# A decoder trunk's state-space scan: real sums on GpSimd, imaginary sums and scans on VectorE

## The chip, the cores and the metric

The kernel runs on one core of a Trainium2 chip. The metric is the device time of one execution in microseconds (us), lower is better; the number given for a kernel is the median of its runs. One execution was also taken by the hardware profiler, and all rows below come from that one.

## What is computed

The reference is a decoder trunk of two layers on 512 tokens of width 1024. Each layer projects its input for three token mixers that stand side by side (windowed attention, a gated delta rule, and a diagonal state space called S5), sums what they give, and then runs an expert network and a gated embedding. The edit is inside S5. There the projected input `u` drives 16 groups of 64 complex states, each with a complex decay:

```python
bu_r = jnp.einsum('blgp,gnp->blgn', uf, bb_r)
bu_i = jnp.einsum('blgp,gnp->blgn', uf, bb_i)
xr, xi = jax.vmap(scan_one)(bu_r, bu_i)      # x[t] = a * x[t-1] + bu[t], complex, along the tokens
y = (jnp.einsum('blgn,gpn->blgp', xr, c_re) - jnp.einsum('blgn,gpn->blgp', xi, c_im) + d_skip * uf)
```

## The kernel before

The states stand on partitions, 128 at a time, which makes 8 blocks a layer (`S5_BLOCKS`); the 512 tokens stand along the free dimension. The hardware's scan is real, and the decay is complex. So the kernel turns the inputs of every token by the angle that the decay has gathered up to it (a table `m.rot`, cosine and sine, made on GpSimd in the phase before), scans the real and the imaginary half separately with the decay's magnitude `m.mag`, and turns the result back.

All of this is in `phase_attend`, together with the windowed attention, with which it shares the engines. The attention has 16 iterations (`N`); its VectorE part is `soft` (L767 to L781): three operations that read scores from PSUM banks (L772, L775, L777) and a maximum (L781). VectorE's order is written out by hand (L822 to L833): `soft(it)`, in some iterations a normalisation, a copy or a skip (L819), and at every odd iteration from 3 to 17 one recurrence, `recur(b)`, for the blocks 0 to 7. The last two recurrences have no `soft` between them. TensorE's order is written out likewise (L700 to L712): the scores one iteration ahead, transposed probabilities, the inputs of a block (`s5_input`, L676), the attention's values, and the outputs of a block (`s5_output`, L683, matmul L688) at the iteration after its recurrence on VectorE. After block 3 and after block 7, VectorE adds the skip term to the finished outputs (L819). ScalarE copies a block's inputs from PSUM to `bu` (L745, L747). GpSimd sets a tile of zeros to zero (L727) and has nothing else in this phase. An all-engine barrier (`clear`) ends the phase.

`recur(b)` has two halves of the same build. In the first, `turn` makes four products of 128x512 in two instructions (L795) into the tile `turned`; L803 adds the real half and L804 subtracts the imaginary half into `ur`; a signal (L805) frees `bu` for ScalarE; then both halves are scanned, the real one first (L807). In the second, `turn` runs on the scanned `z` into the same tile `turned`, L813 and L814 make the two halves of `xs`, and a signal (L815, semaphore `x_ready`) frees TensorE's outputs. `recur(b)` waits for that signal of block b - 1 before it overwrites `turned`.

`step.mark` lets an instruction count up a semaphore when it is done, `step.step` does so and waits for the count, and `sem_inc` is an instruction of its own in the engine's queue that counts up a semaphore for another engine. All tiles are float32 with 128 partitions. The sums and products of a recurrence read two tensors from SBUF each; L772 reads a table of distances from SBUF and the scores from PSUM.

Of the kernel before, what the change touches and what calls it, by code (L numbers as in the profile page):

```python
# [20 lines left out]
ALU = mybir.AluOpType  # L21
# [18 lines left out]
S5_BLOCKS = 8  # L40
# [92 lines left out]
def over(ap, shape):  # L133

    return ap.to_broadcast(list(shape))


def semaphores(m, names):

    names = names.split()  # L140
    while len(m.sems) < len(names):
        m.sems.append(m.ctx.enter_context(m.nc.semaphore(f"phase{len(m.sems)}")))
    return namedtuple("Semaphores", names)(*m.sems[:len(names)])
# [9 lines left out]
COMMON = "landed0 landed1 landed2 params_in act_filled act_read vec_filled vec_read act_step vec_step pool_step"  # L153
# [435 lines left out]
def phase_attend(m, layer):  # L589
# [3 lines left out]

    nc, io = m.nc, m.io
    with ExitStack() as ctx:
        s = semaphores(m, COMMON + " soft_ready exp_done o_filled o_ready ur_ready scanned x_ready y_done y_read gelu_done zeros_set cells_cleared")
        sb = lambda n, shape, dt=F32: ctx.enter_context(nc.sbuf_tensor(f"{n}_{layer}", shape, dt))
        small = sb("small2", [P, 64])
        zeros = sb("zeros", [P, ZEROS])
# [1 line left out]
        ur = sb("s5_ur", [P, 2, T])  # L601
        z = sb("s5_z", [P, 2, T])
        turned = sb("s5_turned", [P, 2, 2, T])
        xs = sb("s5_x", [P, 2, 2, T])
# [24 lines left out]
        def _(pe):  # L629
# [51 lines left out]
                bu_count[b] = to_act.n  # L681

            def s5_output(b):  # L683
                pe.wait_ge(s.x_ready, b + 1)
                if b == 4:
                    pe.wait_ge(s.y_read, 1)
                for part in range(2):
                    ins = nc.tensor.matmul(ybank[:, :], m.s5_out[:, part, b * P:(b + 1) * P], xs[:, b % 2, part, :],  # L688
                                           start=(b % 4 == 0 and part == 0), stop=(b % 4 == 3 and part == 1))
                ins.then_inc(s.y_done, 1)  # L690
# [34 lines left out]
        @block.gpsimd  # L725
        def _(pool):
            nc.gpsimd.memset(zeros[:, :], 0.0).then_inc(s.zeros_set, 1)  # L727

        @block.scalar
        def _(act):  # L730
# [30 lines left out]
        @block.vector  # L761
        def _(v):
            step = Link(v, s.vec_step)
            banks = Reader(v, m.banks[3:6], s.vec_filled, s.vec_read)
            tt, stt = nc.vector.tensor_tensor, nc.vector.scalar_tensor_tensor

            def soft(it):  # L767
                r, sl = it // 4, it % 4
                if it >= 3:
                    v.wait_ge(s.act_filled, pt_count[it - 3])  # L770
                bank = banks.take()
                stt(out=e[it % 3][:, 0:512], in0=m.c("dist_g0")[:, (3 - r) * P:(7 - r) * P], scalar=-float(SLOPES[sl]),  # L772
                    in1=bank[:, :], op0=ALU.mult, op1=ALU.add).then_inc(s.vec_read, 1)
                bank = banks.take()
                step.mark(stt(out=e[it % 3][:, 512:640], in0=m.c("dist_g1"), scalar=-float(SLOPES[SLOTS + sl]),  # L775
                              in1=bank[:, 0:P], op0=ALU.mult, op1=ALU.add))
                stt(out=e[it % 3][:, 640:768], in0=m.c("dist_g2"), scalar=-float(SLOPES[2 * SLOTS + sl]),  # L777
                    in1=bank[:, P:2 * P], op0=ALU.mult, op1=ALU.add).then_inc(s.vec_read, 1)
                banks.settle()
                step.settle()  # L780
                nc.vector.tensor_reduce(nmax[:, it:it + 1], e[it % 3], AX_X, ALU.max, negate=True).then_inc(s.soft_ready, 1)  # L781

            def normalise(r):
                v.wait_ge(s.o_filled, 4 * r + 4)
                if r >= 2:
                    v.wait_ge(s.act_filled, at_count[r - 2])
                step.step(nc.vector.reciprocal(rden[:, 4 * r:4 * r + 4], den[:, 4 * r:4 * r + 4]))
                tt(osb[r % 2].rearrange("p (s c) -> p s c", s=4),
                   obanks[r % 2][:, 0:256].rearrange("p (s c) -> p s c", s=4),
                   over(rden[:, 4 * r:4 * r + 4].unsqueeze(2), (P, 4, HEAD)), ALU.mult).then_inc(s.o_ready, 1)  # L790

            def turn(b, src):

                for n in range(2):
                    step.mark(tt(turned[:, n], src, over(m.rot[:, n, b, :].unsqueeze(1), (P, 2, T)), ALU.mult))  # L795
                step.settle()

            def recur(b):
                v.wait_ge(s.act_read, bu_count[b])
                if b >= 1:  # L800
                    v.wait_ge(s.x_ready, b)
                turn(b, bu[:, b % 2])
                step.mark(tt(ur[:, 0], turned[:, 0, 0], turned[:, 1, 1], ALU.add))  # L803
                step.step(tt(ur[:, 1], turned[:, 0, 1], turned[:, 1, 0], ALU.subtract))  # L804
                v.sem_inc(s.ur_ready, 1)  # L805
                for part in range(2):
                    nc.vector.tensor_tensor_scan(z[:, part, :], over(m.mag[:, b:b + 1], (P, T)), ur[:, part, :],  # L807
                                                 0.0, ALU.mult, ALU.add).then_inc(s.scanned, 1)
                v.wait_ge(s.scanned, 2 * b + 2)
                if b >= 2:  # L810
                    v.wait_ge(s.y_done, b - 1)
                turn(b, z[:, :, :])
                step.mark(tt(xs[:, b % 2, 0], turned[:, 0, 0], turned[:, 1, 1], ALU.subtract))  # L813
                step.step(tt(xs[:, b % 2, 1], turned[:, 0, 1], turned[:, 1, 0], ALU.add))  # L814
                v.sem_inc(s.x_ready, 1)  # L815

            def skip(yt):
                v.wait_ge(s.y_done, 4 * yt + 4)
                stt(out=m.sT[:, yt, :], in0=m.uT[:, yt, :], scalar=m.s5_d[:, yt:yt + 1], in1=ybank[:, :],  # L819
                    op0=ALU.mult, op1=ALU.add).then_inc(s.y_read, 1)  # L820

            for it in range(N + 4):  # L822
                if it < N:
                    soft(it)
                if it >= 3 and (it - 3) % 4 == 3 and (it - 3) // 4 < 4:
                    normalise((it - 3) // 4)
                if it in (11, 19):
                    skip((it - 11) // 8)
                if it - 1 in GATES_AT:
                    bank = banks.take()  # L830
                    nc.vector.tensor_copy(m.ba[:, GATES_AT.index(it - 1), :], bank[:, 0:2 * DN]).then_inc(s.vec_read, 1)
                if it % 2 == 1 and 0 <= (it - 3) // 2 < S5_BLOCKS:
                    recur((it - 3) // 2)  # L833
# [1301 lines left out]
def decoder_trunk(nc, io):  # L2135
    with ExitStack() as ctx:
# [24 lines left out]
        for layer in range(DEPTH):  # L2161
            with ExitStack() as mix:
# [6 lines left out]
                with ExitStack() as own:  # L2169
                    so = lambda n, shape, dt=F32: own.enter_context(nc.sbuf_tensor(f"{n}_{layer}", shape, dt))  # L2170
                    m.mixer_consts = so("mixer_consts", [P, ALWAYS])
                    m.ba = so("ba", [P, NT, 2 * DN])
                    m.w_ba = so("w_ba", [P, KD, 2 * DN])
                    m.conv_w = so("conv_w", [P, 3 * DN, 4])
                    m.a_log = so("a_log", [P, DN])
                    m.dt_bias = so("dt_bias", [P, DN])
                    m.out_gain = so("out_gain", [P, 1])
                    with ExitStack() as front:
                        sf = lambda n, shape, dt=F32: front.enter_context(nc.sbuf_tensor(f"{n}_{layer}", shape, dt))
                        m.work_a = sf("work_a", [P, NT * D])  # L2180
                        m.qkT = m.work_a[:, :].rearrange("p (b n) -> p b n", b=8)
                        m.att_qk = sf("att_qk", [P, 4, QK_HEADS * HEAD])
                        m.att_v = sf("att_v", [P, 4, SLOTS * HEAD])
                        m.uT = sf("uT", [P, 2, T])
                        m.rot = sf("rot", [P, 2, 8, T])
                        m.s5_in = sf("s5_in", [P, 2, 8 * P])
                        m.s5_out = sf("s5_out", [P, 2, 8 * P])
                        m.s5_d = sf("s5_d", [P, 2])
                        m.mag = sf("mag", [P, 8])
                        m.seed = sf("seed", [P, 2, 8])  # L2190
                        phase_project(m, layer)
                        phase_attend(m, layer)
                    phase_deltanet(m, layer)
# [49 lines left out]
```

## Time and profile before

| what | us |
|---|---|
| median of 3 runs | 4196.78 (4196.75 to 4200.75) |
| the profiled execution | 4196.88 |
| its span on the core | 4194.8 |
| VectorE busy in the span | 2647.2 (63%) |
| TensorE busy in the span | 3743.3 (89%) |
| GpSimd busy in the span | 1860.7 (44%) |

The span runs from the first to the last instruction of the program; what lies outside it is 2.1 us. A busy share is a mean over phases with different limits, so the rows below are taken from the stretches that bear on the edit. PE is TensorE, DVE VectorE, ACT ScalarE, POOL GpSimd. In a timeline the first number is an instruction's start in us from the span's start, the second its duration; a mark like x2 merges that many of one line, and brackets give the idle time of the engine before it and what ended it. The engine's pipeline lets an instruction's start overlap the one before it by some 0.1 us. Instructions that only wait or count a semaphore have no row of their own.

### The profile page before, as it was taken

What the parts mean: (1) busy time and instruction counts of PE and PEld (TensorE: products, weight loads), DVE (VectorE), ACT (ScalarE), POOL (GpSimd) and SP (SyncE); (2) the same over time, 40 slices, a digit from 0 to 9 for tenths busy, and PEclk for the clock granted to TensorE, in tenths of its full rate; (3) what the DMA queues carried; (4) which work ended last, traced back from release to release, by engine and by line L of the source; (5) the groups of instructions that cost most, each with busy time, mean ns of one, the idle gap of its engine ahead of it and who ended that gap; (6) DMA issues with size and microseconds to landing.
All of it is one profiled execution on the core that took longest, in us unless ns stands there. A gap on an engine that the chain in (4) does not pass through costs nothing. (4 is left out here: it accounts for less than half of the span.)

```text
span 4194.8 us, 42902 instructions
## 1 busy us (share of the span) xinstructions
PE 3743.3 (89%) x15498; PEld 2766.4 (66%) x15498; DVE 2647.2 (63%) x5548; ACT 734.3 (18%) x1375; POOL 1860.7 (44%) x1714
## 2 busy tenths in 40 slices
PE   8889998978999999994797899989789999999937
PEld 7546787867666666651685467878676666666516
DVE  4766215748677676877657652167486777668776
ACT  2243302212000000000222433022120000000002
POOL 6101103776455455556371020047664554555563
PEclk9889999999999999997898999999899999999968
DMA  3201134548999999999722011445599999999997
GB/s 104 111 30 41 57 137 115 125 120 299 409 409 409 409 402 410 406 409 397 274 83 111 31 41 67 141 119 123 131 311 410 409 406 407 409 408 407 402 391 267
DMA packets 333955, 1063.93 MB, mean 254 GB/s; under 512 B 79152, under 2 KB 96176, under 8 KB 312496
## 3 DMA queue, kind: packets, MB, share of 16 engines
q0 software_dynamic: 184320, 537.08, 34.8%
q1 hardware_dynamic: 132368, 505.22, 31.9%
q10 hardware_dynamic: 17056, 18.88, 1.3%
q8 instruction: 124, 2.03, 0.2%
q14 instruction: 87, 0.71, 0.0%
HBM read 1025.27 MB, written 35.78 MB: 253 GB/s over the span
## 5 line engine op out<-in xcount | busy, mean ns | idle before, releaser
L1665 PE MATMUL bank<-v_tile,shared 128*128 128x512 f32 x2048 | 908.4, 598 | 38.5 <-DVE shared L2041 35.3
L2100 POOL DMA_INDIRECT u_rows<-in_peer_u,idx_all x512 | 645.1, 1260 | 591.9 <-DVE act_u L1998 478.2
L2010 DVE SCALAR_TENSOR_TENSOR x<-v_rows,act_w,x 128x1024 f32<-128x1024 f32 x512 | 657.7, 1285 | 335.2 <-DMA v_rows<-in_peer_v,idx_all 316.9
L2100 POOL DMA_INDIRECT v_rows<-in_peer_v,idx_all x512 | 561.7, 1097 | 423.4 <-DVE x L2010 331.7
L1998 DVE CUSTOM_DVE_ANT_0 u_rows<-u_rows,h 128x1024 f32<-128x1024 f32 x512 | 610.9, 1222 | 189.9 <-DMA u_rows<-in_peer_u,idx_all 187.5
L1665 PEld LDWEIGHTS bank<-v_tile,shared 128*128 128x128 f32 x2048 | 392.5, 192 | 493.1 <-issue 447.2
L2110 POOL DMA_INDIRECT first_cells<-first_gate,cell_all x256 | 417.1, 1629 | 578.5 <-DVEq L1990 462.4
L1653 PE MATMUL bank<-hT,bT 128*128 128x256 f32 x2048 | 452.5, 379 | 0.0
L1653 PEld LDWEIGHTS bank<-hT,bT 128*128 128x128 f32 x2048 | 388.4, 190 | 72.0 <-issue 22.0
L1557 PE MATMUL bank<-hT,ring 128*128 128x256 f32 x1536 | 341.1, 383 | 14.2 <-PEq L150 14.2
L1557 PEld LDWEIGHTS bank<-hT,ring 128*128 128x128 f32 x1536 | 293.6, 192 | 56.5 <-issue 15.8
L1315 POOL TENSOR_TENSOR dn_ct<-dn_lt,mixer_consts 128x512 f32<-128x512 f32 x48 | 64.1, 1335 | 597.2 <-ACT dn_lt L1127 461.7
L1653 PE MATMUL bank<-hT,aT 128*128 128x256 f32 x1024 | 239.3, 388 | 15.4 <-DMA aT<-in_peer_ut 12.4
L1653 PEld LDWEIGHTS bank<-hT,aT 128*128 128x128 f32 x1024 | 198.6, 196 | 60.0 <-issue 29.5
L1846 ACT ACTIVATE shared<-bank 128x512 f32<-128x512 f32 x128 | 76.0, 595 | 918.8 <-PE bank L1665 881.3
L1611 PE MATMUL bank<-hT,ring 128*128 128x256 f32 x1024 | 230.8, 385 | 3.5 <-issue 2.7
L1653 PE MATMUL bank<-hT,sT 128*128 128x256 f32 x1024 | 231.5, 379 | 0.0
L1611 PEld LDWEIGHTS bank<-hT,ring 128*128 128x128 f32 x1024 | 198.0, 194 | 37.2 <-issue 8.6
L1653 PEld LDWEIGHTS bank<-hT,sT 128*128 128x128 f32 x1024 | 194.6, 190 | 26.5
L1896 DVE TENSOR_TENSOR shared<-shared,bank 128x512 f32<-128x512 f32 x48 | 32.5, 686 | 252.3 <-PE bank L1557 250.9
L361 PE MATMUL bank<-ring,hT 128*128 128x256 f32 x640 | 151.4, 398 | 0.0
L361 PEld LDWEIGHTS bank<-ring,hT 128*128 128x128 f32 x640 | 150.1, 329 | 1.0 <-issue 0.5
(375 smaller groups left out, 4749.8 us busy)
## 6 DMA issues: line engine op xcount, KB each, us to landing
v_tile<-in_peer_v SPq DMA_DIRECT2D x256, 512.0 KB, 7.5
ring<-in_w_in_panels SPq DMA_DIRECT2D x76, 1024.0 KB, 4.9
bT<-in_peer_ut SPq DMA_DIRECT2D x128, 512.0 KB, 7.9
ring<-in_peer_w_query SPq DMA_DIRECT2D x32, 1024.0 KB, 5.2
aT<-in_peer_ut SPq DMA_DIRECT2D x64, 512.0 KB, 6.9
sT<-in_peer_ut SPq DMA_DIRECT2D x64, 512.0 KB, 6.8
ring<-in_ple_w_gate SPq DMA_DIRECT2D x24, 1024.0 KB, 6.8
first_cells<-zeros SPq DMA_DIRECT2D x16, 1024.0 KB, 11.1
```

What stands on the lines that cost most here:

```text
L361: ins = nc.tensor.matmul(bank[:, 0:PANEL], m.hT[:, k, r::4], w[:, k, :], start=(k == 0), stop=(k == KD - 1))
L1315: nc.gpsimd.tensor_tensor(heads(ct[:, i % 2, :]), heads(lt[:, i % NT, :]), over(m.c(f"join{JOINS[i // NT]}").unsqueeze(1), (P, DN, P)), AL ...
L1557: ins = mm(bank[:, cols(mt)], a[:, mt * P:(mt + 1) * P], b[:, cols(half)], start=(n == 0), stop=(n == len(groups) - 1))
L1611: ins = mm(bank[:, cols(part)], w[:, k, part * P:(part + 1) * P], m.hT[:, k, cols(half)], start=(k == 0), stop=(k == KD - 1))
L1653: ins = mm(m.banks[2 + p % 2][:, cols(e % 2)], pre_w[e % DENSE][:, k, :], m.hT[:, k, cols(0)], start=(k == 0), stop=(k == KD - 1))
L1665: ins = mm(acc[t][part][:, :], act_pair[p % AHEAD][:, at:at + P], v_tile[:, e % DENSE, part * 512:part * 512 + 512], start=(e == 0), stop= ...
L1846: f(act_pair[p % AHEAD], m.banks[2 + p % 2][:, :], ACT.Gelu_apprx_tanh).then_inc(s.pre_read, 1)
L1896: tt(sig[:, br, :], sig[:, br, :], bank[:, :], ALU.mult).then_inc(s.vec_read, 1)
L1998: nc.vector.tensor_tensor_reduce(out=u[:, n % RINGS, :], in0=u[:, n % RINGS, :], in1=h[:, t, :], scale=1.0, scalar=0.0, op0=ALU.mult, op1= ...
L2010: stt(out=m.x[:, 2 + t, :], in0=vr[:, n % RINGS, :], scalar=act_w[:, p % 4, i:i + 1], in1=m.x[:, 2 + t, :], op0=ALU.mult, op1=ALU.add).the ...
L2100: nc.gpsimd.indirect_dma_start(out=rows[:, n % RINGS, :], out_offset=None, in_=table, in_offset=bass.IndirectOffsetOnAxis(ap=idx_all[:, t, ...
L2110: nc.gpsimd.indirect_dma_start(out=cells, out_offset=bass.IndirectOffsetOnAxis(ap=cell_all[:, n:n + 1], axis=0), in_=first_gate[:, 0, n:n ...
```

## The change

In each half of a recurrence, VectorE no longer makes the real sum. It counts up a new semaphore, `rotated`, when the products are done, and makes the imaginary sum. GpSimd waits for `rotated` and makes the real sum from the same tile `turned`. In the first half VectorE scans the imaginary half first, and waits for GpSimd's `ur_pooled` before it scans the real half. In the second half `x_ready` is counted up by both engines, so TensorE's output of a block, and VectorE's next overwriting of `turned`, wait for a count of two a block.

```diff
--- before.py
+++ after.py
@@ -593,7 +593,7 @@
 
     nc, io = m.nc, m.io
     with ExitStack() as ctx:
-        s = semaphores(m, COMMON + " soft_ready exp_done o_filled o_ready ur_ready scanned x_ready y_done y_read gelu_done zeros_set cells_cleared")
+        s = semaphores(m, COMMON + " soft_ready exp_done o_filled o_ready ur_ready scanned x_ready y_done y_read gelu_done zeros_set cells_cleared rotated ur_pooled")
         sb = lambda n, shape, dt=F32: ctx.enter_context(nc.sbuf_tensor(f"{n}_{layer}", shape, dt))
         small = sb("small2", [P, 64])
         zeros = sb("zeros", [P, ZEROS])
@@ -681,7 +681,7 @@
                 bu_count[b] = to_act.n
 
             def s5_output(b):
-                pe.wait_ge(s.x_ready, b + 1)
+                pe.wait_ge(s.x_ready, 2 * b + 2)
                 if b == 4:
                     pe.wait_ge(s.y_read, 1)
                 for part in range(2):
@@ -725,6 +725,11 @@
         @block.gpsimd
         def _(pool):
             nc.gpsimd.memset(zeros[:, :], 0.0).then_inc(s.zeros_set, 1)
+            for b in range(S5_BLOCKS):
+                pool.wait_ge(s.rotated, 2 * b + 1)
+                nc.gpsimd.tensor_tensor(ur[:, 0], turned[:, 0, 0], turned[:, 1, 1], ALU.add).then_inc(s.ur_pooled, 1)
+                pool.wait_ge(s.rotated, 2 * b + 2)
+                nc.gpsimd.tensor_tensor(xs[:, b % 2, 0], turned[:, 0, 0], turned[:, 1, 1], ALU.subtract).then_inc(s.x_ready, 1)
 
         @block.scalar
         def _(act):
@@ -798,19 +803,21 @@
             def recur(b):
                 v.wait_ge(s.act_read, bu_count[b])
                 if b >= 1:
-                    v.wait_ge(s.x_ready, b)
+                    v.wait_ge(s.x_ready, 2 * b)
                 turn(b, bu[:, b % 2])
-                step.mark(tt(ur[:, 0], turned[:, 0, 0], turned[:, 1, 1], ALU.add))
+                v.sem_inc(s.rotated, 1)
                 step.step(tt(ur[:, 1], turned[:, 0, 1], turned[:, 1, 0], ALU.subtract))
                 v.sem_inc(s.ur_ready, 1)
-                for part in range(2):
+                for part in (1, 0):
+                    if part == 0:
+                        v.wait_ge(s.ur_pooled, b + 1)
                     nc.vector.tensor_tensor_scan(z[:, part, :], over(m.mag[:, b:b + 1], (P, T)), ur[:, part, :],
                                                  0.0, ALU.mult, ALU.add).then_inc(s.scanned, 1)
                 v.wait_ge(s.scanned, 2 * b + 2)
                 if b >= 2:
                     v.wait_ge(s.y_done, b - 1)
                 turn(b, z[:, :, :])
-                step.mark(tt(xs[:, b % 2, 0], turned[:, 0, 0], turned[:, 1, 1], ALU.subtract))
+                v.sem_inc(s.rotated, 1)
                 step.step(tt(xs[:, b % 2, 1], turned[:, 0, 1], turned[:, 1, 0], ALU.add))
                 v.sem_inc(s.x_ready, 1)
```

## Rows read from the trace of the kernel before

**Rows 1.** Part 1 of the page, the whole span: busy us, share, instructions of each engine.
```profile
PE 3743.3 (89%) x15498; PEld 2766.4 (66%) x15498; DVE 2647.2 (63%) x5548; ACT 734.3 (18%) x1375; POOL 1860.7 (44%) x1714
```

**Rows 2.** Busy us by stretch, both layers: PE, PEld, DVE, ACT, POOL, PEclk.
```profile
139.50:257.50 118.00, 94.58 (x457) 64.76 (x456) 104.94 (x143) 31.41 (x60) 0.00 (x0) 0.86 0.17 62
2228.60:2345.80 117.20, 95.26 (x458) 64.70 (x456) 105.01 (x143) 31.15 (x59) 0.00 (x0) 0.85 0.18 65
```

**Rows 3.** Groups by line, VectorE, 139.5 to 257.5 us: busy, mean ns | idle.
```profile
L772 DVE SCALAR_TENSOR_TENSOR att_qk<-mixer_consts,bank 128x512 f32<-128x512 f32 x12 | 8.2, 685 | 2.9 <-PE bank L639 1.6 <-DVE s_x L814 1.3
L819 DVE SCALAR_TENSOR_TENSOR sT<-uT,s_d,bank 128x512 f32<-128x512 f32 x2 | 1.5, 748 | 6.8 <-PE bank L688 6.8
```

**Rows 4.** Timeline of VectorE, first recurrence: start us, us, instruction, idle before and releaser.
```profile
139.51 2.35 DVE L795 TENSOR_TENSOR s_turned<-s_bu,rot 128x1024 f32<-128x1024 f32 x2
141.89 0.69 DVE L803 TENSOR_TENSOR s_ur<-s_turned 128x512 f32<-128x512 f32 x1
142.50 0.69 DVE L804 TENSOR_TENSOR s_ur<-s_turned 128x512 f32<-128x512 f32 x1
143.33 2.34 DVE L807 TENSOR_TENSOR_SCAN s_z<-mag,s_ur 128x512 f32<-128x512 f32 x2
145.71 2.36 DVE L795 TENSOR_TENSOR s_turned<-s_z,rot 128x1024 f32<-128x1024 f32 x2
148.71 0.68 DVE L814 TENSOR_TENSOR s_x<-s_turned 128x512 f32<-128x512 f32 x1
149.61 0.69 DVE L772 SCALAR_TENSOR_TENSOR att_qk<-mixer_consts,bank 128x512 f32<-128x512 f32 x1 [0.22 <-DVE s_x L814]
```

**Rows 5.** Timeline of TensorE, first layer's recurrences.
```profile
150.35 2.07 PE L639 MATMUL bank<-work_a 64*128 64x512 f32 x2 [3.39 <-DVE att_qk L772]
158.75 1.94 PE L688 MATMUL bank<-s_x,s_out 128*128 128x512 f32 x4
242.82 1.98 PE L688 MATMUL bank<-s_x,s_out 128*128 128x512 f32 x4 [1.42 <-DVEq L815]
252.97 3.52 PE L688 MATMUL bank<-s_x,s_out 128*128 128x512 f32 x4 [7.32 <-DVEq L815]
```

**Rows 6.** Timeline of VectorE, seventh recurrence's end and eighth's start.
```profile
242.03 0.68 DVE L814 TENSOR_TENSOR s_x<-s_turned 128x512 f32<-128x512 f32 x1
242.96 2.36 DVE L795 TENSOR_TENSOR s_turned<-s_bu,rot 128x1024 f32<-128x1024 f32 x2
```

**Rows 7.** Timelines of VectorE and GpSimd, phase of the delta rule, 353.7 us.
```profile
353.66 0.69 DVE L1232 TENSOR_TENSOR dn_l<-dn_l,mixer_consts 128x512 f32<-128x512 f32 x1 [0.97 <-ACT dn_lt L1127]
354.27 1.77 DVE L1233 TENSOR_TENSOR dn_xt<-dn_lt,mixer_consts 128x512 f32<-128x512 f32 x1
...
353.71 1.77 POOL L1315 TENSOR_TENSOR dn_ct<-dn_lt,mixer_consts 128x512 f32<-128x512 f32 x1 [227.71 <-ACT dn_lt L1127]
```

**Rows 8.** The same two timelines at 376 us.
```profile
376.95 0.42 DVE L1266 TENSOR_TENSOR dn_l<-dn_l,bank 128x256 f32<-128x256 f32 x1 [0.22 <-DVEq L1236]
377.29 0.41 DVE L1266 TENSOR_TENSOR dn_xt<-dn_xt,bank 128x256 f32<-128x256 f32 x1
...
376.14 1.72 POOL L1315 TENSOR_TENSOR dn_ct<-dn_lt,mixer_consts 128x512 f32<-128x512 f32 x1 [2.73 <-PE bank L999]
```

**Rows 9.** The same two timelines at 369 us.
```profile
369.20 1.75 DVE L1232 TENSOR_TENSOR dn_l<-dn_l,mixer_consts 128x512 f32<-128x512 f32 x1
...
369.14 1.27 POOL L1315 TENSOR_TENSOR dn_ct<-dn_lt,mixer_consts 128x512 f32<-128x512 f32 x1 [8.95 <-PE bank L999]
```

**Rows 10.** The same two timelines at 358.9 us.
```profile
358.89 0.17 DVE L1250 COPY small<-dn_er 128x4 f32<-128x4 f32 x1 [0.17 <-DVE dn_l L1243]
...
358.89 1.30 POOL L1315 TENSOR_TENSOR dn_ct<-dn_lt,mixer_consts 128x512 f32<-128x512 f32 x1 [3.40 <-ACT dn_lt L1127]
```

**Rows 11.** Timelines of VectorE and GpSimd in the projection phase, 29 us.
```profile
29.29 0.17 DVE L484 COPY seed<-s_small 128x8 f32<-128x8 f32 x1
...
29.54 0.20 POOL L568 TENSOR_TENSOR rot_tmp<-rot,seed 128x4 f32<-128x4 f32 x1 [19.98 <-DVE seed L484]
```

## The prediction

> **What bounds the kernel now.** I started from the busy shares of the whole span [rows 1], and they do not help: the edit touches one phase, the attention and state-space phase, which runs once per layer. So I read the busy time of that stretch in each layer [rows 2]. VectorE works 105 of 118 us there, TensorE 95 and ScalarE 31; GpSimd does nothing. A busy TensorE need not be the limit, so I asked who waits for whom. In the stretch that holds the first layer's recurrences VectorE's waits for TensorE's scores come to 1.6 us in all, and those for the output matmuls to 6.8, in two places, one of them the tail [rows 3]. TensorE in turn waits for VectorE: its scores of 150.35 could start only when VectorE had read the bank (L772 ended at 149.61 + 0.69 = 150.30) [rows 4, 5]. The loop is paced by VectorE, so a shorter or longer recurrence moves the phase's end one for one, and so the next phase's start, which lies behind a barrier. The layers' stretches are alike [rows 2], and I work out one and double it.
>
> **One recurrence before.** Let E be the end of the first turn, 139.51 + 2.35 = 141.86 [rows 4]. The real sum starts at E + 0.03, the imaginary one ends at 143.19 = E + 1.33, and with the signal to ScalarE between them the scans start at 143.33 = E + 1.47. A signal thus costs VectorE 0.14 from the end of one instruction to the start of the next. Let F be the end of the second turn, 145.71 + 2.36 = 148.07. The last sum ends at 149.39 = F + 1.32, and the next iteration's scores are read from 149.61 = F + 1.54. Each half has two sums of 0.61 to 0.69 us; the change leaves VectorE one of the two, and adds a signal in front of it.
>
> **Can the two engines add at once?** Nothing runs on GpSimd in this phase, so the nearest rows are those of the next phase, where GpSimd's only elementwise work is L1315, the same shape and two inputs in SBUF. Alone it takes 1.27 us [rows 9]. Where VectorE's L1232, also two SBUF inputs, started 0.05 us before it, it took 1.77: it ended at 355.48, 1.13 after VectorE's sum (354.35). VectorE's next two-input sum then took 1.77 in place of 0.69, and ended 0.56 after GpSimd [rows 7]. Where GpSimd started first, by 0.06, it took its 1.27 and VectorE's sum took 1.75, ending 0.54 after it [rows 9]. So these instructions exclude each other, whole instruction by whole instruction, with some 0.13 us of overlap at a change-over. The sums that the code puts side by side will stand one behind the other, and the one moved to GpSimd is twice as long as it was.
>
> An operation with one input in PSUM is not held: L1266 took 0.42 and 0.41 us in the middle of GpSimd's 1.72 [rows 8]. L772, the first thing after a recurrence, also reads one input from PSUM, so I let it run beside GpSimd at no cost. If it were held as well, each second half below would end 0.77 later, 9 us over twelve of them.
>
> **Who is first.** VectorE starts its own sum 0.14 us after the turn ends, as above. GpSimd started 0.09 after VectorE's L484 ended, when it waited for that alone (29.46 to 29.54) [rows 11]; a signal by a separate instruction comes about 0.06 later than one by the instruction itself (TensorE started 0.11 after the end of L814, and 0.05 after the end of L772) [rows 4 to 6]. That makes 0.15 for GpSimd against 0.14: a tie within the trace's resolution. In the one tie the rows show, both at 358.89, VectorE's small copy took its usual 0.17 and GpSimd's L1315 1.30, 0.03 more than alone [rows 10]. So I take VectorE first.
>
> **The sum, VectorE first.**
> - First half: VectorE's sum runs from E + 0.14 to E + 0.83. GpSimd's ends 1.13 later, at E + 1.96. The scan of the imaginary half is ready to start at E + 0.97. Whether a scan is held is shown by no row, since none runs beside GpSimd: free, it starts at E + 0.97; held like the sums of [rows 7], it gets going 0.13 before GpSimd's end, at E + 1.83. I take held, because L807 too reads two tensors from SBUF (the decay and the sums) [rows 4]. Against E + 1.47 that is +0.36 us (free: -0.50). The real half's scan finds its sum done in both cases, so scanning the imaginary half first buys nothing more.
> - Second half: VectorE's sum ends at F + 0.83 and the next iteration starts 0.22 later, at F + 1.05, against F + 1.54: -0.49 us, six times a layer. GpSimd's difference is done at F + 1.96 in place of F + 1.32. TensorE asks for the first one only at 158.75, nine us later [rows 5], so the delay is covered.
> - In two places it is not covered. The eighth recurrence follows the seventh with only a tiny copy between, and its first turn may overwrite the products only when GpSimd has read them. The turn started 0.25 after the last sum (242.71 to 242.96) [rows 6], F + 1.57; now it starts some 0.09 after GpSimd, F + 2.05: +0.48. And the last output matmul, for which TensorE has waited 7.32 us [rows 5], and behind which the phase ends, starts later by about 0.58.
>
> One layer: 8 x 0.36 - 6 x 0.49 + 0.48 + 0.58 = 2.88 - 2.94 + 1.06 = +1.0 us; both, +2.0. The profiled execution took 4196.88 us (its span 4194.8), 0.1 above the median of 4196.78, so the forecast is **4198.9 us**, no change that can be told: a measurement of this kernel can tell about 0.2%, 8.4 us.
>
> The page "SBUF — State Buffer" of the Trainium skill (section "SBUF: two separate sides") says that VectorE and GpSimd contend for one pair of ports as for a lock, that a VectorE operation with two SBUF inputs takes part, and that whichever starts first holds it for the whole instruction. By that class the scan is held too and the sum is the +2.0 above; if it applied only to the two-tensor sums shown in the rows, the sum would be -11.8 (second rival). No row here shows which.
>
> **Rivals.**
> 1. GpSimd gets in first. The tie is close enough. Then GpSimd runs from E + 0.14 to E + 1.41, VectorE's sum ends 0.54 later [rows 9] at E + 1.95, and the scans start at E + 2.09: +0.62. The second half loses the same, 1.95 + 0.22 = F + 2.17 against F + 1.54. Sixteen halves of 0.62 a layer make 9.9, both layers 19.8: 4216.7, slower. Against it stands the tie of [rows 10], for it that its VectorE operation is a copy of four columns and not a sum. A second half that goes over costs 1.12 us and a first half 0.26, so the time passes +8.4 when a good third of them do. By the page's words on whichever starts first, a GpSimd that starts earlier by the least bit would give this time.
> 2. The scans are free. Then the first half gains 0.50 and a layer has 6 x -0.99 - 0.02 + 0.08 = -5.9; both, -11.8: 4185.1. A faster VectorE would meet TensorE's own work sooner (95 of 118 us) [rows 2], which could take some of it back.
> 3. No exclusion between these instructions, the two sums truly side by side: GpSimd done at E + 1.41, under the first scan; -0.99 six times, about -0.5 in each of the last two recurrences, -6.9 a layer: 4183.1. Every collision in the rows speaks against it.
>
> **How the numbers follow.** Forecast, VectorE mostly first and the scans held: 0.61. GpSimd first in more than a third of the halves: 0.29. Free scans: 0.07. No exclusion: 0.03. A tenth of a us in each of the 32 halves is 3 us either way, so the forecast's own range is 4195 to 4203; 4196.8, where nothing would have moved, lies in it. With the first rival and two us above it the range is 4194 to 4219; it leaves out the two fast cases, 0.10. Faster by over 0.2% are those two, 0.10; within 0.2% is the forecast, 0.61; slower by over 0.2% is the first rival, 0.29.
>
> **What would show it.** After the change GpSimd has 16 sums a layer. Right, each lasts about 1.8 us in place of 1.27, VectorE's sums keep 0.69, the first scan of each recurrence lasts about 2.1 in place of 1.2, and L772 starts some 1.05 after the second turn's end. With the first rival VectorE's sums last 1.8 and GpSimd's 1.27. With free scans the first scan keeps 1.2; without exclusion every one keeps its time. The forecast is wrong if the order goes over to GpSimd, or if L772 stretches beside it.

## The result, and the profile after

The changed kernel took 4213.51 us in the median of 8 runs (4209.83 to 4216.84), the kernel before beside it 4200.23 (4196.75 to 4202.44, 8 runs): a ratio of 1.0032 [1.0021, 1.0043], 13.3 us slower. Run once more later it gave 1.0044 [1.003, 1.0059], 17.9 us slower. The time lies in the predicted range, but not where the likeliest case put it: what came is the first rival, GpSimd first.

The profiled execution took 4213.98 us, its span 4211.9. First the first recurrence on VectorE, to be held against [rows 4] (the lines have moved by 5 to 7: the turn is L800, the sums L809 and L821, the scans L814, the first read of the scores L777):

```profile
139.81 2.35 DVE L800 TENSOR_TENSOR s_turned<-s_bu,rot 128x1024 f32<-128x1024 f32 x2
142.30 1.80 DVE L809 TENSOR_TENSOR s_ur<-s_turned 128x512 f32<-128x512 f32 x1
144.25 2.34 DVE L814 TENSOR_TENSOR_SCAN s_z<-mag,s_ur 128x512 f32<-128x512 f32 x2
146.63 2.36 DVE L800 TENSOR_TENSOR s_turned<-s_z,rot 128x1024 f32<-128x1024 f32 x2
149.13 1.80 DVE L821 TENSOR_TENSOR s_x<-s_turned 128x512 f32<-128x512 f32 x1
151.16 0.69 DVE L777 SCALAR_TENSOR_TENSOR att_qk<-mixer_consts,bank 128x512 f32<-128x512 f32 x1 [0.22 <-DVE s_x L821]
```

The same stretch on GpSimd:

```profile
142.29 1.26 POOL L730 TENSOR_TENSOR s_ur<-s_turned 128x512 f32<-128x512 f32 x1 [16.19 <-DVEq L808]
149.12 1.26 POOL L732 TENSOR_TENSOR s_x<-s_turned 128x512 f32<-128x512 f32 x1 [5.57 <-DVEq L820]
```

GpSimd's sum starts 0.01 us ahead of VectorE's and takes what it takes alone. VectorE's, 0.69 in [rows 4], now takes 1.80 and ends 0.55 after GpSimd's. Taking one of two sums from VectorE made the other longer than both had been. The scans keep their 2.34 for the pair: by the time they start, GpSimd is done. The groups of the stretch from 139.5 to 257.5 us (busy us, mean ns of one | idle before) show that this is every half and not the first alone:

```profile
L809 DVE TENSOR_TENSOR s_ur<-s_turned 128x512 f32<-128x512 f32 x8 | 14.4, 1805 | 1.2
L821 DVE TENSOR_TENSOR s_x<-s_turned 128x512 f32<-128x512 f32 x7 | 12.6, 1801 | 1.0
L730 POOL TENSOR_TENSOR s_ur<-s_turned 128x512 f32<-128x512 f32 x8 | 10.1, 1266 | 70.7 <-DVEq L808 70.7
L732 POOL TENSOR_TENSOR s_x<-s_turned 128x512 f32<-128x512 f32 x7 | 8.9, 1265 | 39.0 <-DVEq L820 39.0
```

The busy shares of the two layers' stretches, in the columns of [rows 2]:

```profile
139.50:257.50 118.00, 94.53 (x452) 65.09 (x450) 107.62 (x121) 31.12 (x58) 18.98 (x15) 0.82 0.17 63
2228.60:2345.80 117.20, 98.32 (x472) 67.59 (x470) 102.41 (x121) 34.24 (x65) 16.46 (x13) 0.82 0.21 79
```

VectorE is as busy as before (107.6 and 102.4 us, where [rows 2] has 104.9 and 105.0), though half of its sums went to another engine, and GpSimd's 19.0 and 16.5 us are all new. (The stretches keep their times, and the late work has moved past their ends: 121 instructions of VectorE, where 143 less the 16 sums would be 127.) A wait for another engine's use of SBUF counts as busy time in these records: no idle gap points to it, only a mean duration that has grown.

Where each layer's next phase begins is told by one fill, L1173 before and L1180 after. Before:

```profile
260.69 0.09 DVE L1173 MEMSET dn_raw<- 128x36 f32 x1 [3.42 <-PEq L150]
2349.27 0.09 DVE L1173 MEMSET dn_raw<- 128x36 f32 x1 [3.52 <-PEq L150]
```

After:

```profile
270.47 0.09 DVE L1180 MEMSET dn_raw<- 128x36 f32 x1 [3.65 <-PEq L150]
2368.26 0.09 DVE L1180 MEMSET dn_raw<- 128x36 f32 x1 [3.64 <-PEq L150]
```

It is 9.78 us late in the first layer and 18.99 in the second, where the rival's sum gives 9.9 and 19.8; at the span's end 17.1 are left.

### The profile page after: what moved, and what is told of

Read it like the earlier page. It is cut to its first block and busy times, and to the rows that moved or that the text cites. A ratio compares the mean times of both kernels' runs of the same rounds, so it can differ in the third digit from the quotient of the medians.

```text
span 4211.9 us, 42934 instructions
## 1 busy us (share of the span) xinstructions
PE 3749.4 (89%) x15498; PEld 2770.3 (66%) x15498; DVE 2665.7 (63%) x5516; ACT 736.1 (17%) x1375; POOL 1924.7 (46%) x1746
## 5 line engine op out<-in xcount | busy, mean ns | idle before, releaser
L2107 POOL DMA_INDIRECT u_rows<-in_peer_u,idx_all x512 | 653.7, 1277 | 582.6 <-DVE act_u L2005 462.8
L2107 POOL DMA_INDIRECT v_rows<-in_peer_v,idx_all x512 | 577.2, 1127 | 408.8 <-DVE x L2017 311.6
L1564 PEld LDWEIGHTS bank<-hT,ring 128*128 128x128 f32 x1536 | 292.6, 191 | 56.1 <-issue 15.8
```

The costliest lines, as they stand in the source:

```text
L1564: ins = mm(bank[:, cols(mt)], a[:, mt * P:(mt + 1) * P], b[:, cols(half)], start=(n == 0), stop=(n == len(groups) - 1))
L2107: nc.gpsimd.indirect_dma_start(out=rows[:, n % RINGS, :], out_offset=None, in_=table, in_offset=bass.IndirectOffsetOnAxis(ap=idx_all[:, t, ...
```

## The experiments

The theory: VectorE's and GpSimd's sums exclude each other, GpSimd gets in first each time, and each half of a recurrence so grows by 0.62 us. Against it stood these: the added signals cost it; the new waits or the turned order of the scans do; any instruction of GpSimd gets in VectorE's way, whatever it reads; the two sums get in each other's way because both read the tile `turned`. Runs 1 to 4 shared a chip and their runs of the kernel before, and so did 6 to 8; run 5 came last, on another chip and with runs of the kernel before of its own.

**1. VectorE first.** VectorE issues its own sum ahead of the signal. Against the changed kernel (the second half alike):

```diff
                 turn(b, bu[:, b % 2])
+                step.mark(tt(ur[:, 1], turned[:, 0, 1], turned[:, 1, 0], ALU.subtract))
                 v.sem_inc(s.rotated, 1)
-                step.step(tt(ur[:, 1], turned[:, 0, 1], turned[:, 1, 0], ALU.subtract))
+                step.settle()
```

> VectorE's own sum is issued ahead of the signal to GpSimd, nothing else is changed against the changed kernel. Theory (two-input operations of the two engines exclude each other, and GpSimd won by a hair): VectorE's sums keep 0.69 us, GpSimd's take about 1.8 (they end 1.13 after VectorE's). If the scan is held too, the first scan lasts about 2.2 us and gets going 1.72 us after the turn's end: +0.25 in a first half, -0.60 in six second halves, +0.4 and +0.5 in the last two: -1.5 us in all against the kernel before, some 15 to 20 below the changed kernel. If the scan is free, the first scan keeps 1.2 us and the kernel ends 15 below the one before. Rival (the loss comes from the signals and waits, whoever is first): the changed kernel's time, about 13 above the one before.

Measured: 4197.02 us against 4197.55, ratio 1.0 [0.999, 1.0009]. The loss is gone. Groups of the same stretch:

```profile
L815 DVE TENSOR_TENSOR_SCAN s_z<-mag,s_ur 128x512 f32<-128x512 f32 x16 | 25.4, 1628 | 1.2
L730 POOL TENSOR_TENSOR s_ur<-s_turned 128x512 f32<-128x512 f32 x8 | 13.6, 1704 | 62.1 <-DVEq L809 62.1
L808 DVE TENSOR_TENSOR s_ur<-s_turned 128x512 f32<-128x512 f32 x8 | 5.5, 692 | 0.3
```

Now VectorE's sum has its 0.69 and GpSimd's takes 1.70. The scans' mean rose from 1212 to 1628 ns, and it is one of each pair that grew: the first takes 2.06 us, the second 1.19. So a scan is held by GpSimd's sum, as the forecast took it; the second rival is out. The scan reads `mag` and `ur` where GpSimd reads `turned`, so the two engines need not read the same tile.

**2. The second half only.** GpSimd makes the real difference of the second half; the first half is as before, with no turned scans and no wait between them. Against the kernel before, beside the counts of `x_ready`:

```diff
+            for b in range(S5_BLOCKS):
+                pool.wait_ge(s.rotated, b + 1)
+                nc.gpsimd.tensor_tensor(xs[:, b % 2, 0], turned[:, 0, 0], turned[:, 1, 1], ALU.subtract).then_inc(s.x_ready, 1)
...
-                step.mark(tt(xs[:, b % 2, 0], turned[:, 0, 0], turned[:, 1, 1], ALU.subtract))
+                v.sem_inc(s.rotated, 1)
```

> Both first sums and the order of the scans are again as in the kernel before; GpSimd makes only the real difference of the second half. Theory (0.62 us lost in every half alike, by exclusion with GpSimd first): 16 x 0.62 = +9.9 us against the kernel before; L821's successor 1.8 us in all 16 places. Rival (the loss sits in the scan's wait for GpSimd and the turned order of the scans): about 0.

Measured: 4205.65 against 4197.55, ratio 1.0019 [1.0009, 1.0029], +8.1 us. Groups:

```profile
L817 DVE TENSOR_TENSOR s_x<-s_turned 128x512 f32<-128x512 f32 x8 | 14.4, 1800 | 1.2
L730 POOL TENSOR_TENSOR s_x<-s_turned 128x512 f32<-128x512 f32 x8 | 10.1, 1262 | 122.3 <-DVEq L816 122.3
L806 DVE TENSOR_TENSOR s_ur<-s_turned 128x512 f32<-128x512 f32 x8 | 5.5, 692 | 0.3
```

Half of the edit makes about half of the loss, and only the sum with a partner on GpSimd is long. Neither the order of the scans nor the wait between them is needed for it.

**3. The signals alone.** The kernel before with the two added signals, and nothing moved:

```diff
                 turn(b, bu[:, b % 2])
+                v.sem_inc(s.rotated, 1)
                 step.mark(tt(ur[:, 0], turned[:, 0, 0], turned[:, 1, 1], ALU.add))
...
                 turn(b, z[:, :, :])
+                v.sem_inc(s.rotated, 1)
                 step.mark(tt(xs[:, b % 2, 0], turned[:, 0, 0], turned[:, 1, 1], ALU.subtract))
```

> The kernel before with the two added signals in each recurrence and no work on GpSimd. Theory: a signal puts 0.11 us between the products and the first sum, 32 x 0.11 = +3.5 us, so it is a fifth of the loss. Rival (the signals are the loss): +13 or more.

Measured: 4199.72 against 4197.55, ratio 1.0006 [0.9996, 1.0016]: +2.2 us, within the measurement. In the timeline the turn ends at 139.50 + 2.35 = 141.85 and the sum starts 0.14 later, in place of 0.03:

```profile
139.50 2.35 DVE L795 TENSOR_TENSOR s_turned<-s_bu,rot 128x1024 f32<-128x1024 f32 x2
141.99 0.69 DVE L804 TENSOR_TENSOR s_ur<-s_turned 128x512 f32<-128x512 f32 x1
```

The signals are 0.11 us each, 3.5 in all, and not the 13 to 18.

**4. GpSimd without reads.** In the changed kernel GpSimd fills the same tiles with zeros at the same places. This leaves out the real sums.

```diff
-                nc.gpsimd.tensor_tensor(ur[:, 0], turned[:, 0, 0], turned[:, 1, 1], ALU.add).then_inc(s.ur_pooled, 1)
+                nc.gpsimd.memset(ur[:, 0], 0.0).then_inc(s.ur_pooled, 1)
...
-                nc.gpsimd.tensor_tensor(xs[:, b % 2, 0], turned[:, 0, 0], turned[:, 1, 1], ALU.subtract).then_inc(s.x_ready, 1)
+                nc.gpsimd.memset(xs[:, b % 2, 0], 0.0).then_inc(s.x_ready, 1)
```

> GpSimd's sums are replaced by setting the same tiles to zero: it writes SBUF at the same places behind the same signals and reads none, so the real halves are left out of the computation. If the exclusion is about reading two tensors: VectorE's sums keep 0.69 us, each half is 0.5 us shorter than in the kernel before, 32 x 0.49 = -15.7 us. If any GpSimd operation excludes VectorE's: each sum waits for GpSimd's 0.52 us and ends 0.55 after it, a half is then 0.12 shorter, -4 us. If the waits were the loss and not the exclusion: +13 as in the changed kernel.

Measured: 4179.6 against 4197.55, ratio 0.9955 [0.9938, 0.9971], -18 us. All signals, waits and the turned scans of the change are in this kernel. Groups:

```profile
L821 DVE TENSOR_TENSOR s_x<-s_turned 128x512 f32<-128x512 f32 x8 | 5.5, 692 | 1.2
L809 DVE TENSOR_TENSOR s_ur<-s_turned 128x512 f32<-128x512 f32 x8 | 5.5, 692 | 1.2
L730 POOL MEMSET s_ur<- 128x512 f32 x8 | 4.2, 525 | 71.4 <-DVEq L808 71.4
```

A fill of 0.53 us that started 0.03 ahead of VectorE's sum left it at 0.69. GpSimd's writes of a whole half do not hold it; the sum that reads two tensors does. No run has elementwise work of GpSimd with a single input. The page "SBUF — State Buffer" of the Trainium skill (section "SBUF: two separate sides") says just this of VectorE's operations with two SBUF inputs: they lock only against an operation of GpSimd that reads SBUF. Runs 1, 2 and 4 agree: GpSimd's sum takes 1.70 in run 1, VectorE's takes 1.80 in run 2 and 0.69 here.

**5. GpSimd a little later.** The question left was what decides who is first. In the changed kernel, one small fill on GpSimd ahead of each sum, and nothing altered on VectorE:

```diff
                 pool.wait_ge(s.rotated, 2 * b + 1)
+                nc.gpsimd.memset(late[:, :], 0.0)
                 nc.gpsimd.tensor_tensor(ur[:, 0], turned[:, 0, 0], turned[:, 1, 1], ALU.add).then_inc(s.ur_pooled, 1)
                 pool.wait_ge(s.rotated, 2 * b + 2)
+                nc.gpsimd.memset(late[:, :], 0.0)
```

> The changed kernel with one small fill (128x1) on GpSimd between each signal and its sum, and nothing altered on VectorE: GpSimd's sum starts some 0.05 to 0.1 us later than in the changed kernel, so after VectorE's own sum instead of 7 to 11 ns before it. If the start alone decides which of the two holds the other, the order flips: VectorE's sum takes 0.69 us, GpSimd's 1.7 to 1.8, the first scan starts 0.85 us after the turn's products end and takes about 2.1, the soft work starts 1.05 us after the products of the second half end instead of 2.17. That is the course that the prediction took for the likeliest, +2 us against the kernel before, worked out there; about -15 to -17 against the changed kernel. If GpSimd goes ahead however the starts lie, or the loss is in the waits: VectorE's sum stays at 1.8 or more and the time at +13 to +22.

Measured: 4198.55 against 4198.8 (11 and 15 runs), ratio 0.9998 [0.9989, 1.0007]. VectorE's timeline:

```profile
138.68 2.35 DVE L803 TENSOR_TENSOR s_turned<-s_bu,rot 128x1024 f32<-128x1024 f32 x2
141.18 0.69 DVE L812 TENSOR_TENSOR s_ur<-s_turned 128x512 f32<-128x512 f32 x1
142.01 3.18 DVE L817 TENSOR_TENSOR_SCAN s_z<-mag,s_ur 128x512 f32<-128x512 f32 x2
145.23 2.36 DVE L803 TENSOR_TENSOR s_turned<-s_z,rot 128x1024 f32<-128x1024 f32 x2
147.74 0.69 DVE L824 TENSOR_TENSOR s_x<-s_turned 128x512 f32<-128x512 f32 x1
148.65 0.69 DVE L780 SCALAR_TENSOR_TENSOR att_qk<-mixer_consts,bank 128x512 f32<-128x512 f32 x1 [0.22 <-DVE s_x L824]
```

and GpSimd's:

```profile
141.15 0.10 POOL L731 MEMSET s_late<- 128x1 f32 x1 [15.69 <-DVEq L811]
141.21 1.79 POOL L732 TENSOR_TENSOR s_ur<-s_turned 128x512 f32<-128x512 f32 x1
```

GpSimd's sums start 27 to 30 ns after VectorE's in all 32 halves, where in the changed kernel they start 7 to 11 ns before in all 32 (differences of the trace's time stamps, finer than the timelines print), and with that every half has gone over. A little extra work on the engine that was too early wins 14 to 18 us back.

**6. Second half of the first six recurrences, VectorE first.** The rest of the recurrence is as before the change:

```diff
+                if b < S5_BLOCKS - 2:
+                    step.mark(tt(xs[:, b % 2, 1], turned[:, 0, 1], turned[:, 1, 0], ALU.add))
+                    v.sem_inc(s.rotated, 1)
+                    step.settle()
+                    v.sem_inc(s.x_ready, 1)
+                    return
                 step.mark(tt(xs[:, b % 2, 0], turned[:, 0, 0], turned[:, 1, 1], ALU.subtract))
```

> Only the real sum of the second half of the recurrences 0 to 5 goes to GpSimd, and VectorE issues its own sum ahead of the signal, so that it is first. If the loss is the order alone: VectorE's sum 0.69 us, GpSimd's about 1.7, the soft work 0.95 us after the turn instead of 1.54, so -0.6 for 12 recurrences, about -7 us against the kernel before. If GpSimd is first or what follows on VectorE is held all the same: +0.6 for 12, about +7 us.

Measured: 4190.32 (11 runs) against 4198.05, ratio 0.9979 [0.997, 0.9989], -7.7 us. GpSimd's sums take a mean of 1705 ns, VectorE's 692. This is the part of the change that pays.

**7. Both sums of the second half.** GpSimd makes both, one after the other, in the first six recurrences, and VectorE goes straight on:

```diff
+            for b in range(S5_BLOCKS - 2):
+                pool.wait_ge(s.rotated, b + 1)
+                nc.gpsimd.tensor_tensor(xs[:, b % 2, 0], turned[:, 0, 0], turned[:, 1, 1], ALU.subtract).then_inc(s.x_ready, 1)
+                nc.gpsimd.tensor_tensor(xs[:, b % 2, 1], turned[:, 0, 1], turned[:, 1, 0], ALU.add).then_inc(s.x_ready, 1)
...
+                if b < S5_BLOCKS - 2:
+                    v.sem_inc(s.rotated, 1)
+                    return
```

> GpSimd makes both second-half sums of the recurrences 0 to 5 of a layer, one after the other (about 1.26 us each, 2.5 together), and VectorE goes straight on to the soft work of the next operand; the first halves and the last two recurrences are as before the change. If exclusion needs a partner that reads two SBUF tensors, and the soft operations, which read PSUM or one tensor, are no such partner: the first soft operation starts some 0.25 us after the products of the turn end instead of 1.54 us after, so 1.3 us less for 12 recurrences, about -15.6 us against the kernel before; the recurrence's result is ready some 1.4 us later, which the slack of TensorE's wait for it (5.7 us at the least in these recurrences) takes in. If any work of VectorE is held while GpSimd reads: the soft work waits for both sums, 2.5 us, about +1.2 for 12, +14 us.

Measured: 4175.99 against 4198.05, ratio 0.9951 [0.9937, 0.9965], -22.1 us: faster than both kernels. VectorE, from the second turn on:

```profile
145.74 2.36 DVE L799 TENSOR_TENSOR s_turned<-s_z,rot 128x1024 f32<-128x1024 f32 x2
148.32 0.69 DVE L776 SCALAR_TENSOR_TENSOR att_qk<-mixer_consts,bank 128x512 f32<-128x512 f32 x1 [0.22 <-DVE s_turned L799]
148.92 0.28 DVE L779 SCALAR_TENSOR_TENSOR att_qk<-mixer_consts,bank 128x128 f32<-128x128 f32 x1
149.12 0.28 DVE L781 SCALAR_TENSOR_TENSOR att_qk<-mixer_consts,bank 128x128 f32<-128x128 f32 x1
149.43 0.95 DVE L785 TENSOR_REDUCE small<-att_qk 128x1 f32<-128x768 f32 x1
```

and GpSimd beside it:

```profile
148.23 1.27 POOL L730 TENSOR_TENSOR s_x<-s_turned 128x512 f32<-128x512 f32 x1 [22.30 <-DVEq L818]
149.46 1.26 POOL L731 TENSOR_TENSOR s_x<-s_turned 128x512 f32<-128x512 f32 x1
```

For 2.5 us GpSimd reads two tensors from SBUF, and VectorE works through four operations beside it at their usual times: three with one input in PSUM, and a maximum (L785) with a single input in SBUF. Neither side is held. The start moved from F + 1.54 to F + 0.22, 1.32 us twelve times, 15.8; the medians gave 22.1. In the profiled execution the next phase began 8.8 us earlier in the first layer and 18.6 in the second (7.9 and 15.8 by that sum), and the end came 20.9 earlier. Counted from the start of each layer's first turn to that phase, the stretch is 8.8 and 8.3 us shorter, 1.3 more than the sum; the other 3.8 lie in stretches that the edit does not touch, and no run took them apart.

**8. The changed kernel again.**

> The changed kernel once more, unedited, for the size of the loss. By the trace each of the 32 halves is 0.62 us longer, 19.8 us in all, of which the profiled execution kept 17.1; the first comparison of medians gave 13.3 us. If the granted clock gives some of it back in most executions, the median stays at +12 to +17; if the first comparison was low by chance, +17 to +20.

Measured: 4215.93 (5 runs) against 4198.05, +17.9 us. In its profile the fill that opens the next phase comes 14.1 us late in the first layer, where the first profile had 9.8. Most of the difference is there before any recurrence: the first turn of this execution starts at 143.25 us, that of the first profile at 139.81. The stretch from 128 to 139.5 us, in the columns of [rows 2], first in the first profile and then in the second:

```profile
128.00:139.50 11.50, 11.50 (x44) 6.58 (x42) 7.45 (x16) 4.76 (x10) 0.00 (x0) 0.75 0.84 338
```

```profile
128.00:139.50 11.50, 11.50 (x28) 6.26 (x26) 5.69 (x12) 3.63 (x7) 0.00 (x0) 0.50 0.83 334
```

TensorE is busy throughout in both. It was granted a mean clock of 0.75 in the first and 0.50, the lower of its two levels of 1.2 and 2.4 GHz, in the second, where it got through 28 matmuls in place of 44. So the same program was 3.4 us apart before the changed code had run. The place of a phase's end in one execution is thus uncertain by some us, while the length of a half is not: it is 0.62 longer in both.

## Why the prediction was right or wrong

All halves in one table, from the first recurrence of each profile. E and F are the ends of the two turns as in the prediction; the columns give the time from E to the end of both scans and from F to the next read of the scores.

| kernel | E to scans' end, us | F to next scores, us | medians, us |
|---|---|---|---|
| before | 3.81 | 1.54 | |
| changed | 4.43 | 2.17 | +13.3, +17.9 |
| 1, VectorE first | 4.05 | 0.95 | -0.5 |
| 5, GpSimd a little later | 4.16 | 1.06 | -0.3 |
| 3, signals alone | 3.92 | 1.66 | +2.2 |
| 4, no reads | 3.32 | 1.06 | -18 |
| 2, second half only | 3.81 | 2.17 | +8.1 |
| 6, second half, VectorE first, six times | 3.81 | 0.95 | -7.7 |
| 7, both second sums, six times | 3.81 | 0.22 | -22.1 |

The measured time lies in the range because the first rival was counted into it; the likeliest case, 4198.9 us, did not come.

- **The exclusion was right**, and its prices were. With GpSimd first, the prediction put the scans' start at E + 2.09 and the next scores at F + 2.17; the changed kernel shows 144.25 - 142.16 = 2.09 and 151.16 - 148.99 = 2.17. With VectorE first, it put the scans' end 0.36 later and the scores at F + 1.05; run 5 shows 0.35 and 1.06. "I take held", of the scan, was right by run 1. That L772 runs "beside GpSimd at no cost" was right by run 7.
- **The step that failed is "So I take VectorE first."** It had GpSimd's start at 0.15 after the turn against VectorE's 0.14, called that a tie, and let [rows 10] decide it. The starts that came are 0.136 to 0.138 and 0.144 to 0.147: VectorE's estimate was exact and GpSimd's 0.014 too late, and that changed the sign. [Rows 10] was read rightly and was not the same tie. There too the copy goes first: GpSimd's L1315 ends 1.13 after it, as it does after a sum in [rows 7]. But the two start within 6 ns of each other, by the time stamps: in the ten profiles of this case such a pair comes 20 times, in some with GpSimd up to 5 ns ahead, and the copy keeps its 0.17 every time. GpSimd's lead in the changed kernel is 7 to 11 ns. Whether a sum loses at the same lead as a copy, no run shows; the prediction named this doubt ("a copy of four columns and not a sum") and still gave the row the vote.
- That a copy of one tensor takes part at all was already in the profile before, where the projection phase has L525, once a layer, beside GpSimd's L568, with no tile in common. In the first layer GpSimd starts first, in the second the copy:

```profile
47.60 0.61 POOL L568 TENSOR_TENSOR rot_tmp<-rot,rot_w 128x256 f32<-128x256 f32 x1
47.77 0.59 DVE L525 COPY qk_gain<-qk_gain 128x256 f32<-128x256 f32 x1
```

```profile
2137.11 0.29 DVE L525 COPY qk_gain<-qk_gain 128x256 f32<-128x256 f32 x1
2137.21 0.66 POOL L568 TENSOR_TENSOR rot_tmp<-rot,rot_w 128x256 f32<-128x256 f32 x1
```

  The copy that comes second takes 0.59 in place of 0.29 and ends 0.15 after GpSimd. So the maximum of run 7 does not stand for every operation with one input in SBUF.
- The forecast's own case is a true description of a kernel, only not of this one: run 5, which is the change with GpSimd 0.04 us later, has each of its rows and its time (-0.3 where it said +2.0, both within the 8.4 that can be told). The gap between forecast and rival, 17.8 us in the prediction, was 14 to 18 between that kernel and the changed one.
- **A chance of 0.29 for the first rival was too low** for a difference of 0.01 us in a sum of two estimates, each known to 0.01 or 0.02. With no row to tell on which side of the tie this kernel would fall, the two cases stood about even, and a tie that a program meets the same way 32 times goes the same way 32 times: the case "in more than a third of the halves" was in truth all or nothing.
- **"One for one" was nearly right.** Counted from the start of a layer's first turn to the fill of the next phase, the stretch grew by 9.5 and 12.2 us in the first profile and by 10.3 and 10.2 in the second, where the rival's sum has 9.9. Outside these stretches some was won back: in the first profile 2.9 us between the two and 1.9 after the later one. The medians kept 13.3 and 17.9 of 19.8; their intervals, 8.8 to 18.1 and 12.6 to 24.8 us, overlap. What wins it back was not taken apart: run 8 shows that the same program, at another granted clock, can be 3.4 us apart before the changed code has run.
- The third rival, no exclusion, is out by every run in which GpSimd reads; run 4 shows what it would have given, -18 us, where it said -13.8, with VectorE's course in the first recurrence as it had it (0.49 earlier in the first half, and F + 1.06). Like run 7 it gained 4 to 6 us more than its halves add up to.

## What to carry to other kernels

Before work is shared out to GpSimd beside VectorE, list for each operation what it reads. While GpSimd adds or multiplies two tensors from SBUF, VectorE's sum of two tensors, its scan and its copy from SBUF to SBUF (L525) take turns with it by whole instructions, and the order decides whether the half given away costs (run 2: +8.1 us) or saves (run 6: -7.7 us). Give GpSimd such work where VectorE's next operations read PSUM or take the maximum of a single tensor (run 7: -22.1 us); where both must add at once, make the shorter engine's instruction start first by program order, not by luck (run 1). When two estimates are closer than their errors, no neighbouring row of another kind of instruction breaks the tie: give both orders the same chance, and look at what decides them.

## What was not expected

- A few ns decide: with GpSimd 7 to 11 ns earlier VectorE loses every half, with GpSimd 27 to 30 ns later it wins every half, and 14 to 18 us lie between.
- A signal set off by a separate instruction on VectorE lets GpSimd start 0.136 us after the turn, ahead of the signaller's own next instruction at 0.145. In all 32 halves VectorE, which signals first and then computes, is second.
- The scan takes part in the exclusion: 2.06 us beside GpSimd's sum against 1.2 alone. It also takes over with an overlap: in run 1 it ends 1.08 after GpSimd, about 0.14 less than its own time. The page "SBUF — State Buffer" of the Trainium skill (section "SBUF: two separate sides") says that whoever starts first has the ports for the whole instruction and the other is fully blocked; runs 1 and 5 agree on the order, and these records show the change-over 0.13 to 0.15 us before the first one's recorded end.
- GpSimd's fills take no part: 0.53 us beside a two-input sum of VectorE, which keeps its 0.69.
